# Sparse attention: heads' values made before the attention, and head outputs taken on two column halves

## The reference, cut to what matters

```python
SEQ = 512; A_HEADS = 8; HEAD_DIM = 64; A_V_LATENT = 128; Q_BLOCK = 128
# dsa_attention, per block of 128 queries (4 blocks)
p = jax.nn.softmax(logits, axis=-1)              # over the chosen keys
o_lat = jnp.einsum('bthk,btkc->bthc', p, vg)     # vg: chosen latent values, 128 wide, shared by all heads
o = jnp.einsum('bthc,hcd->bthd', o_lat, w_uv)    # up-projection of each head, 128 -> 64
# then: merged = sigmoid(gate_a) * (y_a @ w_o_a) + sigmoid(gate_b) * (y_b @ w_o_b)
```

## Time and profile before

| | |
|---|---|
| median of 3 runs | 2257.8 us (2257.65 to 2258.45) |
| profiled execution, its own time | 2256.78 us |
| its span | 2255.1 us |
| PE, DVE, ACT, POOL busy | 98%, 48%, 36%, 41% of the span |
| mean granted PE clock | 0.998 of full speed |

### The profile page before, as it was taken

One profiled execution on the slowest core, in us unless ns is written; L12 is line 12 of the kernel. 1 busy time (PEld: TensorE's weight loads), 2 busy tenths in 40 slices (PEclk: granted clock), 3 DMA queues, 4 the chain that ended last, 5 costly groups with the idle time before them and its releaser, 6 DMA issues.

```text
span 2255.1 us, 30104 instructions
## 1 busy us (share of the span) xinstructions
PE 2214.4 (98%) x12106; PEld 1786.5 (79%) x12106; DVE 1071.7 (48%) x1508; ACT 801.4 (36%) x825; POOL 935.1 (41%) x509
## 2 busy tenths in 40 slices
PE   8999999999999999999999999999999999999998
PEld 6888888776666888888888788787878878888887
DVE  5423202675753353332045451647566546888701
ACT  4222313437744242223142542433333244222313
POOL 4555544443321445554444244323233343444443
PEclk9999999999999999999999999999999999999999
DMA  4223323343332232232233113313121243323132
GB/s 153 94 93 100 90 98 103 81 75 61 63 111 94 93 103 94 93 102 93 93 104 94 57 58 104 101 38 95 57 76 57 86 149 103 94 93 105 63 102 84
DMA packets 162169, 203.36 MB, mean 90 GB/s; under 512 B 12236, under 2 KB 117015, under 8 KB 162071
## 3 DMA queue, kind: packets, MB, share of 16 engines
q1 hardware_dynamic: 155296, 197.16, 28.9%
q10 hardware_dynamic: 6775, 4.80, 0.7%
HBM read 191.45 MB, written 10.49 MB: 90 GB/s over the span
## 4 chain that ended last, share of the span: by engine, by line
PE 84%; DVE 7%; issue 5%; ACT 3%; POOL 1%; DMA 0%; ACTq 0%; POOLq 0%; DVEq 0%
PE PS L213 23%; PE PS L215 22%; PE PS L214 22%; PE PS L244 2%; PE PS L246 2%; PE PS L245 2%; POOL wl L204 1%; DVE work L2409 1%; PE PS L1134 1%; PE PS L1674 1%; PE PS L1231 1%; PE PS L2176 1%; PE PS L2159 1%; DVE work L2412 1%; DVE work L2421 1%
## 5 line engine op out<-in xcount | busy, mean ns | idle before, releaser
L204 POOL TENSOR_TENSOR wl<-raw,wh 128x1024 fp32r<-128x1024 f32 x335 | 856.3, 2571 | 1214.6 <-ACT wh L193 1214.6
L213 PE MATMUL PS<-h_hi,wh 128*128 128x512 f32 x1696 | 676.2, 399 | 5.7 <-ACT stage_a L863 3.1
L215 PE MATMUL PS<-h_hi,wl 128*128 128x512 f32 x1696 | 661.1, 390 | 0.0
L214 PE MATMUL PS<-h_lo,wh 128*128 128x512 f32 x1696 | 660.8, 390 | 0.0
L193 ACT ACTIVATE wh<-raw 128x2048 fp32r<-128x2048 f32 (+1 forms) x214 | 332.6, 1554 | 836.8 <-PE PS L215 790.6
L213 PEld LDWEIGHTS PS<-h_hi,wh 128*128 128x128 f32 x1696 | 318.5, 188 | 87.9 <-issue 17.6
L215 PEld LDWEIGHTS PS<-h_hi,wl 128*128 128x128 f32 x1696 | 318.3, 188 | 67.3
L214 PEld LDWEIGHTS PS<-h_lo,wh 128*128 128x128 f32 x1696 | 318.8, 188 | 61.8 <-issue 0.7
L694 DVE SCALAR_TENSOR_TENSOR xT<-PS,xT 128x512 f32<-128x512 f32 x40 | 27.2, 688 | 379.6 <-PE PS L215 379.5
L213 PE MATMUL PS<-act_hi,wh 128*128 (+1 forms) x528 | 205.9, 390 | 1.0 <-POOL wl L204 1.0
L215 PE MATMUL PS<-act_hi,wl 128*128 (+1 forms) x528 | 205.4, 389 | 0.0
(11 more groups left out here) (450 smaller groups left out, 2818.9 us busy)
## 6 DMA issues: line engine op xcount, KB each, us to landing
raw<-in_w_in_dram SPq DMA_DIRECT2D x94, 512.0 KB, 4.6
raw<-in_w_up_dram SPq DMA_DIRECT2D x82, 512.0 KB, 4.6
raw<-in_w_down_dram SPq DMA_DIRECT2D x132, 256.0 KB, 2.8
raw<-in_w_gate_dram SPq DMA_DIRECT2D x42, 512.0 KB, 3.8
raw<-in_w_in_dram SPq DMA_DIRECT2D x20, 256.0 KB, 3.7
raw<-in_w_out_dram SPq DMA_DIRECT2D x16, 256.0 KB, 2.8
raw<-in_w_ret_br_dram SPq DMA_DIRECT2D x8, 512.0 KB, 4.2
gates<-stage SPq DMA_DIRECT2D x16, 256.0 KB, 5.5
```

What stands on the lines that cost most here:

```text
L204: ins = nc.gpsimd.tensor_tensor(wl[:, slot, part], raw[:, slot, part], wh[:, slot, part].bitcast(F32), ALU.subtract)
L213: nc.tensor.matmul(dst, sh, mh, start=start, stop=False)
L214: nc.tensor.matmul(dst, sh, ml, start=False, stop=False)
L215: return nc.tensor.matmul(dst, sl, mh, start=False, stop=stop)
```

## The change

`PE` takes two new asides in unit u1+7: after the 7th product `turn_latent`, four transposes of the latent values into bank 0, and after the 11th `head_values`, four fp32 matmuls of 512 columns, transposed latents (`latT`) against the weights `wuv` of all eight heads, into banks 0 to 3. ACT evacuates `latT` and the four results, which overwrite `pn` (512 columns = 8 heads * 64), ahead of `kbT`. Unit u1+8 waits for these evacuations bank by bank. In the sparse stage the quad's product takes each head's 64 values directly: per key tile four matmuls of 64 output rows and 128 columns, two heads on the two column halves of the array in turn. The up-projection L1244, the copy `olT` and their waits go. Semaphores: `a_o` is now set at the end of the quad's product, one step earlier.

```diff
-        unit_T(pe, u1 + 7, 1, 4, 4, 4, h_hi, h_lo, False, True, (h_ready, H_DONE[1] + KD))
-        pe.wait_ge(qi_set, 1)
-        unit_N(pe, u1 + 8, 0, 0, 4, h_hi, h_lo, True, False)
+        unit_T(pe, u1 + 7, 1, 4, 4, 4, h_hi, h_lo, False, True, (h_ready, H_DONE[1] + KD),
+               asides={6: lambda: turn_latent(pe), 10: lambda: head_values(pe)})
+        unit_N(pe, u1 + 8, 0, 0, 4, h_hi, h_lo, True, False, free=(m1_act, by_act("wv0")[1] - 1))
...
+    def turn_latent(pe):
+        pe.wait_ge(qi_set, 1)
+        for t in range(NT):
+            ins = pe.transpose(PS[:, 0, t * P:(t + 1) * P], pn[:, t, 320:448], ident[:, :])
+        ins.then_inc(lat_T, 1)
+    def head_values(pe):
+        pe.wait_ge(wuv_in, 16)
+        pe.wait_ge(*by_act("lat"))
+        for t in range(NT):
+            nc.tensor.matmul(PS[:, t, :], latT[:, t * P:(t + 1) * P], wuv[:, :, :], start=True, stop=True).then_inc(wv_mm, 1)
...
     def sparse_pe(pe):
-        pe.wait_ge(wuv_in, 16)
...
-                for j in range(tiles_seen):
-                    ins = nc.tensor.matmul(PS[:, 6, :], pn[:, j, 320:448], pT[:, j, :], start=j == 0, stop=j == tiles_seen - 1)
-                ins.then_inc(a_ol, 1)
+                for pair in range(2):
+                    for j in range(tiles_seen):
+                        for h in (2 * pair, 2 * pair + 1):
+                            r, v = PER * (h % 2), (4 * (quad % 2) + h) * PER
+                            ins = nc.tensor.matmul(PS[r:r + 64, 6, pair * P:(pair + 1) * P], pn[:, j, v:v + PER],
+                                                   pT[:, j, h * P:(h + 1) * P], start=j == 0, stop=j == tiles_seen - 1,
+                                                   skip_group_check=True)
+                ins.then_inc(a_o, 1)
...
-            if n >= 5 and n % 4 == 1:
-                quad = n // 4 - 1
-                pe.wait_ge(a_olev, quad + 1)
-                for hh in range(4):
-                    r = PER * (hh % 2)
-                    ins = nc.tensor.matmul(PS[r:r + PER, 6, (hh // 2) * P:(hh // 2 + 1) * P], wuv[:, 4 * (quad % 2) + hh, :],
-                                           olT[:, hh * P:(hh + 1) * P], start=True, stop=True)
-                ins.then_inc(a_o, 1)
...
     # sparse_dve
-            if n >= 4 and n % 4 == 0:
-                dve.wait_ge(a_ol, n // 4)
-                dve.tensor_copy(olT[:, :], PS[:, 6, :]).then_inc(a_olev, 1)
...
     # mid1_act, after rounds(act, u1 + 8, 1)
+        act.wait_ge(lat_T, 1)
+        act.activation(latT[:, :], PS[:, 0, :], ACT.Copy).then_inc(m1_act, 1)
+        for t in range(NT):
+            act.wait_ge(wv_mm, t + 1)
+            act.activation(pn[:, t, :], PS[:, t, :], ACT.Copy).then_inc(m1_act, 1)
```

More of the change, by code:

```diff
@@ L718, in two_blocks_kernel @@
     qbT, kbT, vb = stack(R1, ("qbT", [P, 4, T], F32), ("kbT", [P, 4, T], F32), ("vb", [P, NT, 512], F32))
-    lg, pr, pT, olT = stack(R1, ("lg", [P, 2, T], F32), ("pr", [P, 3, T], F32), ("pT", [P, NT, 512], F32),
-                            ("olT", [P, 512], F32))
+    lg, pr, pT = stack(R1, ("lg", [P, 2, T], F32), ("pr", [P, 3, T], F32), ("pT", [P, NT, 512], F32))
     soff = [None, 0, 2 * P, 5 * P, 9 * P]
@@ L746, in two_blocks_kernel @@
         sem("m1_" + s) for s in "consts dma wi_mm wi_ev cqn_set cq_T cq_set kd_set kd_T qa_set qa_T qi_set qi_T sd act".split())
-    M1_ACT = "pn wi_h wiT cq_hi kT qb0 qb1 qb2 qb3 qa_sq kb qi qa vb".split()
+    M1_ACT = "pn wi_h wiT cq_hi kT qb0 qb1 qb2 qb3 qa_sq lat wv0 wv1 wv2 wv3 kb qi qa vb".split()
     def by_act(name):
@@ L754, in two_blocks_kernel @@
         sem("b_" + s) for s in "z ln sp spm acc exp am pv hi lo".split())
-    a_dot, a_relu, a_causal, a_lg, a_lgm, a_exp, a_pr, a_pT, a_pTev, a_ol, a_olev, a_o, a_yhi, a_ylo = (
-        sem("a_" + s) for s in "dot relu causal lg lgm exp pr pT pTev ol olev o yhi ylo".split())
+    a_dot, a_relu, a_causal, a_lg, a_lgm, a_exp, a_pr, a_pT, a_pTev, lat_T, wv_mm, a_o, a_yhi, a_ylo = (
+        sem("a_" + s) for s in "dot relu causal lg lgm exp pr pT pTev latT wv o yhi ylo".split())
     a_rused, wuv_in = sem("a_rused"), sem("wuv_in")
@@ L1029, in mid1_pe @@
         pe.wait_ge(*by_act("qa"))
+    latT = at("latT", [P, T], offset=Y_B + 12 * 1024)
+    def turn_latent(pe):
[8 more added lines that the diff above has]
+            nc.tensor.matmul(PS[:, t, :], latT[:, t * P:(t + 1) * P], wuv[:, :, :], start=True, stop=True).then_inc(wv_mm, 1)
     def turn_q(pe, src):
@@ L1265, in sparse_act @@
                 if n >= 4:
-                    act.wait_ge(a_ol, n // 4)
+                    act.wait_ge(a_o, n // 4)
                 act.activation(pT[:, 0:n // 8 + 1, :], PS[:, 2:3 + n // 8, :], ACT.Copy).then_inc(a_pTev, 1)
```

## The result

The changed kernel takes 2246.51 us (median of 5 runs, 2245.2 to 2247.63) against 2257.8 us (5 runs beside them): ratio 0.995, 95% interval 0.9938 to 0.9961, 11.3 us less. The forecast was 2247.4 with a range of 2243.5 to 2253. Two more series of the same kernel gave 2246.86 and 2247.02.

The account below looks back on a forecast made before the run. PE was taken as the bound, holding 84% of the chain that ended last, plus some stalls from other engines' order. -10.7 - 3.6 + 3.9 = -10.4 us, from 2257.8 to 2247.4 us, range 2243.5 to 2253.

Parts of the forecast that it names:

- PE's work in the stage, -10.7: Sparse stage: L1231 and L1244 remove 22.2 us, 160 half-array passes add 11.5, so PE's own work changes by -10.7 us.
- Stalls, -3.6: Sparse stage: PE's waits shrink by 1.4 + 1.5 + 0.7 = 3.6 us, with bounds of nothing and 6.7.
- The wait for L1436: Sparse stage: PE's 1.5 us wait for DVE's output-gate product, which stood behind the last `olT`, goes.
- the unnamed one: Before 700.72: PE's 1.0 us wait without a releaser, taken as for the last gate evacuation; 0.7 of it goes.
- `stage_a`, said to stay: Sparse stage: 3.1 us of PE's waits, from ACT doing `pT` or an exponential before the evacuation, stay.
- PE waited three times, 1.4 us in all; these go: Sparse stage: PE's three waits for scaled probabilities, 1.4 us in all, go because DVE no longer copies `olT` first.
- a new wait for `pr` or `pT` as large as the old ones: Sparse stage: a listed sign that the prediction is wrong, PE newly waiting for probabilities or their transposes.
- mid1, +3.9: Unit u1+7 in mid1: four transposes (0.4 us) and four fp32 matmuls (3.4) add 3.9 us, none of it hidden.
- Rival A: Sparse stage: stalls move instead of going, only PE's work counts; -6.8 us, 2251.0 us; chance 0.20.
- B: Quad's product: the two halves' weight loads go one after the other in long groups; +13.4 us, 2260.8 us; chance 0.07.
- C: Last query block: the softmax chain becomes the bound; only -2.8 us, 2255.0 us; chance 0.07.
- lower end, 2243.5: Whole kernel: the range's fast end, reached if all of `stage_a`'s 3.1 us goes too.

Follow-up runs that it names:

- pool_pieces: Changed kernel with POOL's low parts of the last six weight units made in pieces of 256 columns instead of 1024: 2245.49 us, ratio 0.9947.
- gate_first: Changed kernel with ACT's evacuation of a finished gate product moved ahead of `pT` and `ya_hi` in its step: 2244.36 us, ratio 0.9942.
- quad_late: Changed kernel with the quad's product one step later, behind that step's transposes and directly ahead of the scores: 2248.71 us, ratio 0.9964.

## Why the prediction was right, point by point

- **PE's work in the stage, -10.7.** Right: about -11.0 by the starts. Groups of 8 and 32 passes came at 0.58 and 1.90 us for forecast 0.6 and 1.9. Alternating halves overlap in long groups, as the shorter rows of L1150 and L1244 had said.
- **Stalls, -3.6.** By the starts they gave 4.3 us, or 15.4 - 10.7 = 4.7 if the work is taken as forecast; so this term was about 1 us too small, for it was added up from the waits as the profile lists them, which miss a part of each. That these listed waits fell by 3.7 (7.4 before, 3.7 after) where 3.6 was forecast is in part luck. The wait for L1436 and the unnamed one went as forecast (1.5 and 0.7). `stage_a`, said to stay, gave 0.7, and `pT` 0.4, which the forecast left out. The step that failed is "PE waited three times, 1.4 us in all; these go". The three went, but a new wait of 0.9 came, which the prediction's last paragraph names as a sign of being wrong ("a new wait for `pr` or `pT` as large as the old ones"). In the new place the scaling fell on a POOL instruction and lasted 2.48 us; pool_pieces removed it. The longest of the old ones was probably of the same kind and not the work of `olT` alone: its scaling lasted 0.95 us where 0.35 is usual and ended 0.15 us after a POOL instruction.
- **mid1, +3.9.** Right to a tenth: 3.93 in the profile, 4.0 alone on the chip. No wait at the asides.
- **Cause of the stall term.** The experiments bear out the mechanism: putting DVE's wait and copy back costs about 6 us of the stage. That is more than the stalls' 4.3 to 4.7. PE now reaches each place sooner, which would explain it, but that was not tested.
- **Rival A** (the stalls only move) is out as the whole account, since the measured time is 4.5 us below its 2251.0 and the stalls come back with DVE's wait and copy. In one place it was right: the new wait of 0.9. **B** is out: a pair costs 0.11 us in groups of 32. **C** is out: the last query block's waits fell too, a step takes 2.7 us there, and DVE's and ACT's busy time stayed near 50 of 95 us.
- **Range.** Its lower end, 2243.5, is 0.8 us below what its stated reason gives (2247.4 - 3.1 = 2244.3). Nothing hangs on it here.
- Sum: -11.0 - 4.3 + 3.9 = -11.4 against a measured -11.3, forecast -10.4.

## What to carry to other kernels

Read from the distance of starts, not from record lengths, what two half-array matmuls cost, and what a group pays on its way in and out; here both held to 0.1 us in groups four times as long. When a product is reassociated, the copy between its two halves may be worth a good part of what the arithmetic is (4.3 us beside 11.0): here an engine with 50% idle time stood in order behind the product, and what was queued behind it held the busy engine. Before a wait is credited to the engine order, look at what else runs in the same moment: the wait of 0.9 us that stayed here belonged to GpSimd.

## What the runs showed of the hardware that was not expected

- The matmul engine starts passes for a free column half while earlier ones still wait for the other half, four of them in the group read here: with all key tiles of one head first, 32 passes took 2.50 us, against 1.90 in alternation and 3.4 in series (32 x 0.107).
- A DVE scaling or copy from SBUF to SBUF that met a GpSimd `tensor_tensor` of 1024 columns ended 0.1 to 0.3 us after that one (2.48 us for 256 columns, otherwise 0.35). With pieces of 256 columns the longest scaling was 0.88 us. The Trainium skill (GPSIMD Engine Reference, "1. Specifications") names an interface to SBUF that GpSimd shares with VectorE; the trace agrees and adds the size. The masking, which reads PSUM, kept its 0.41 us in the kernel before where it fell on the next such GpSimd instruction (at 642.75).
- Single executions hold a short stretch of lower granted clock (0.66 over 4.4 us in gate_first, 0.71 over 5.9 us in the changed kernel's third profile) at the start of the sparse stage, behind PE's wait of 1.8 us for `yb_lo`. The changed kernel's other two profiles have the same wait and no such stretch. It made the third one's stage 1.2 us longer (96.5 against 95.3) and has to be looked for before two profiles are compared.
- A product on column halves between undivided ones paid about 0.16 us for its way in and out (0.10 ahead, 0.06 behind). Directly ahead of products on row halves it paid neither (quad_late).
